# ScalarE copies a chunk's flipped activations before the next chunk's sigmoid, in a decoder layer with 32 experts

## The reference

```python
def clamped_swiglu(gu):
    gate, up = gu[..., :D_FF], gu[..., D_FF:]
    gate = jnp.minimum(gate, SWIGLU_LIMIT)
    up = jnp.clip(up, -SWIGLU_LIMIT, SWIGLU_LIMIT)
    return (up + 1.0) * (gate * jax.nn.sigmoid(gate * SWIGLU_ALPHA))

def expert_block(args):
    xblk, e = args
    act = clamped_swiglu(xblk @ w_gate_up[e] + b_gate_up[e])
    return act @ w_down[e] + b_down[e]
```

## Time and profile before

| what | before |
|---|---|
| median of 3 runs | 1429.55 us (1427.65 to 1431.92) |
| the profiled execution | 1427.33 us, span 1425.6 us |
| TensorE matmul busy | 1286.2 us, 90% of the span |
| VectorE busy | 496.2 us, 35% |
| ScalarE busy | 324.7 us, 23% |
| mean share of granted TensorE clock | 0.958 |
| the main weight queue's packets | 430.86 MB, 74.5% of 16 DMA engines' span |

### The profile page before, as it was taken

The page is one execution under the profiler, slowest core; times in us unless marked ns, Lnnn a source line. Parts: engine busy times, 40 slices in busy tenths (PEclk is TensorE's granted clock), DMA queues, the critical chain, the costliest instruction groups (busy, mean ns, idle before and its releaser), DMA issues.

```text
span 1425.6 us, 33985 instructions
## 1 busy us (share of the span) xinstructions
PE 1286.2 (90%) x12484; PEld 560.1 (39%) x12485; DVE 496.2 (35%) x1476; ACT 324.7 (23%) x649; POOL 299.4 (21%) x348
## 2 busy tenths in 40 slices
PE   6999999959998999999999999888999899988870
PEld 3764544543333434444444333333443333433320
DVE  2002222443334333333333344342334333343337
ACT  2023332221312222222222222221223222222211
POOL 0513332011212212222212112130212212111210
PEclk9999999969999999999999999999999999999995
DMA  9512110224999999999989999998999989999967
GB/s 379 208 59 74 60 74 1 104 83 173 415 386 415 394 413 395 368 365 366 366 366 365 392 418 416 417 416 352 366 367 417 413 362 414 393 417 416 417 248 294
DMA packets 90869, 454.86 MB, mean 319 GB/s; under 512 B 14049, under 2 KB 14489, under 8 KB 55774
## 3 DMA queue, kind: packets, MB, share of 16 engines
q1 hardware_dynamic: 77902, 430.86, 74.5%
q0 software_dynamic: 12512, 22.11, 4.3%
q10 hardware_dynamic: 432, 1.57, 0.3%
HBM read 444.23 MB, written 14.71 MB: 322 GB/s over the span
## 4 chain that ended last, share of the span: by engine, by line
PE 73%; DMA 21%; DVE 3%; issue 1%; ACT 1%; POOL 0%; SPq 0%; DVEq 0%; POOLq 0%
PE bank L661 35%; DMA arena<-in_w_gate_up 20%; PE bank L687 14%; PE bank L421 7%; PE bank L491 4%; PE bank L437 3%; PE bank L648 2%; PE bank L626 2%; PE bank L706 1%; PE bank L450 1%; DVE xs L1284 1%; PE bank L478 1%; PE bank L464 1%; PE bank L707 1%; PE bank L616 1%
## 5 line engine op out<-in xcount | busy, mean ns | idle before, releaser
L661 PE MATMUL bank<-arena,hT 128*32 128x512 f32 x5120 | 583.9, 606 | 30.2 <-DMA arena<-in_w_gate_up 27.9
L687 PE MATMUL bank<-arena,hT 128*32 128x256 f32 x5120 | 308.4, 386 | 33.1 <-ACT hT L859 33.1
L661 PEld LDWEIGHTS bank<-arena,hT 128*32 128x32 f32 x5120 | 157.3, 111 | 393.0 <-issue 341.1
L1241 DVE TENSOR_TENSOR arena<-bank,gain 128x512 f32<-128x512 f32 x128 | 88.4, 691 | 402.0 <-PE bank L661 402.0
L687 PEld LDWEIGHTS bank<-arena,hT 128*32 128x32 f32 x5120 | 159.6, 111 | 161.3 <-issue 77.3
L963 POOL DMA_DIRECT2D ahead<-in_consts x98 | 51.6, 530 | 641.1 <-DVE hT L1260 615.3
L876 ACT ACTIVATE arena<-arena 128x256 f32<-128x256 f32 x128 | 53.3, 417 | 560.1 <-DVE arena L1243 558.7
L1260 DVE TENSOR_TENSOR hT<-bank,gain 128x256 f32<-128x256 f32 x128 | 51.4, 422 | 212.2 <-PE bank L687 206.1
L980 POOL DMA_INDIRECT y_rows<-hT,arena x80 | 82.4, 1029 | 158.3 <-DVE hT L1260 150.7
L421 PE MATMUL bank<-hT,arena 128*128 128x512 f32 x224 | 103.6, 610 | 0.8 <-ACT hT L764 0.8
L966 POOL DMA_INDIRECT hT<-h_rows,arena x82 | 84.8, 1035 | 67.9 <-issue 34.0
(11 more groups left out here) (146 smaller groups left out, 857.9 us busy)
## 6 DMA issues: line engine op xcount, KB each, us to landing
arena<-in_w_gate_up SPq DMA_DIRECT2D x256, 1024.0 KB, 6.6
arena<-in_w_down SPq DMA_DIRECT2D x128, 1024.0 KB, 15.3
arena<-in_w_in SPq DMA_DIRECT2D x10, 1024.0 KB, 18.1
arena<-y_rows SPq DMA_DIRECT2D x8, 1024.0 KB, 12.3
arena<-in_w_out SPq DMA_DIRECT2D x4, 1024.0 KB, 22.0
arena<-bias_by_dist POOLq DMA_DIRECT2D x6, 512.0 KB, 4.0
xs<-in_x SPq DMA_DIRECT2D x4, 512.0 KB, 7.4
h_rows<-arena POOLq DMA_DIRECT2D x4, 512.0 KB, 2.9
```

The source lines that it names most:

```text
L661: mm = pe.matmul(bank[c][j * CH:(j + 1) * CH, :].rearrange("p (g n) -> p g n", g=2), xT[:, c, (k % 2) * P + (k // 2) * CH:(k % 2) * P + (k ...
L687: mm = pe.matmul(bank[c][j * CH:(j + 1) * CH, 0:Q], aT[:, c, (k % 2) * P + (k // 2) * CH:(k % 2) * P + (k // 2 + 1) * CH], w[:, j * Q:(j + ...
L1241: dve.tensor_tensor(gu[:, b, :], bank[c][:, :], bt[:, 0:2 * Q], ALU.add).then_inc(gu_read, 1)
```

## The change

In ScalarE's loop over chunks, the copy of the flipped activations of chunk n - 1 stands ahead of the sigmoid of chunk n, in place of behind it. Nothing else differs; the copy of the last chunk (n = 3) still follows the loop.

```diff
                 for n, c in enumerate(ORDER):
+                    if n >= 1:
+                        copy_act(job, n - 1)
                     act.wait_ge(gate_clamped, job * NCH + (n + 1))
                     act.activation(sg[:, c % 2, :], gu[:, c % 2, 0:Q], ACT.Sigmoid, scale=ALPHA)\
                         .then_inc(sig_done, 1)
-                    if n >= 1:
-                        copy_act(job, n - 1)
                 copy_act(job, NCH - 1)
```

## The result

| | before | after |
|---|---|---|
| median of 11 runs each, taken together | 1427.14 us (1421.17 to 1431.92) | 1433.05 us (1426.63 to 1437.48) |
| ratio | | 1.0046, 95% interval 1.0025 to 1.0067 |
| the profiled execution's span | 1425.6 us | 1428.8 us |

The kernel is 0.46% slower, about 6 us (3.6 to 9.6 us by the interval). The profiled executions are only 3.2 us apart, since the first unit load of the job loop happens to be issued 2.55 us earlier after, behind stages that the change doesn't touch. From there to the end it takes 5.8 us more.

What follows compares the result with a forecast made beforehand. The prediction had TensorE's matmuls and weight transfers bound the loop in turns. It summed 1427.33 - 1.47 (last job) + 1.57 (one clock fall) = 1427.4, plus 2.2 for the runs' median, 1429.6 us; range 1424.0 to 1436.0.

Steps and rivals of the forecast that it cites:

- five places: Ends of full-queue stretches before three-chunk jobs, with no clock fall before; their waits would grow to 2.8 to 3.1 us.
- slower rival: TensorE's clock falls at most of the five places, costing 7.9 to 10.7 less 1.47 us: 1436.0 to 1438.8 us; chance 0.14.
- half-clock stretches behind several of the eight landings: Sign of being wrong: TensorE at 1.2 GHz behind several landings that end full-queue stretches, with a time near 1436.
- (a): ScalarE: three 0.37 us copies move ahead of sigmoids and delay none, with 1.4 us of cover; price nothing.
- (b): TensorE, two-chunk jobs: the 2.05 us copy wait goes, a flip wait of some 0.5 us comes; 1.47 us gained, 16 times.
- (c): Of 16 gains on TensorE, full weight transfers hide 15; only the last job's 1.47 us reaches the end.
- the landing of the eighth gate unit stays where it is: In full-queue stretches this weight landing doesn't move, so TensorE waits there 1.47 us more; gain 0 for 15 jobs.
- (d): Longer TensorE waits for the eighth unit may bring its clock down: 1.25 falls or five, 7.9 to 10.7 us for five.
- one fall at 1.57 us: The clock term taken into the sum, between ends of no fall and five falls.
- The chain's three places: Rival: all three copies on the profile's chain count, 7.7 us faster, 1421.9 us; chance 0.07.
- the full 23.5 us: Rival: all 16 TensorE waits count, needing a queue that TensorE's down pace moves: 1406.1 us; chance 0.03.
- No effect at all: Rival: TensorE's wait comes back in full at the flip, with neither gain nor new falls: 1429.55 us; chance 0.06.

Runs made afterwards that it cites:

- e1_chunk1_alone: Kernel before, with only chunk 1's copy (the third) moved ahead of a sigmoid: 1433.31 us, ratio 1.0044.
- e5: Kernel before, loading only half of each gate-and-up unit from the second job on, so outputs are not the reference's: 1386.29 us.
- e6: Changed kernel, loading only half of each gate-and-up unit from the second job on, so outputs are not the reference's: 1350.86 us.
- e8: Kernel before, with GpSimd's gathers held until VectorE has read the gate of chunk 1: 1426.01 us, ratio 1.0004.
- e12: Changed kernel with 2.8 us of unread matmuls ending two-chunk jobs, as in e7, and gathers held: 1427.09 us, ratio 0.9994.
- e2: Changed kernel, with about 1.5 us of unread matmuls on TensorE where two-chunk jobs had waited for the copy: 1427.62 us, ratio 1.0006.
- e3: Changed kernel, with about 1.5 us of unread matmuls behind down(0), ending two-chunk jobs: 1427.55 us, ratio 1.0008.
- e7: Changed kernel, with about 2.8 us of unread matmuls behind down(0), ending two-chunk jobs: 1425.05 us, ratio 0.9995.
- e9: Changed kernel, first job written out, unread matmuls filling waits for gate units 6 and 7 behind two-chunk jobs: 1443.9 us, ratio 1.0117.
- e10: Control for e9: same added code, but one 16-column matmul in each of the two places: 1441.14 us, ratio 1.0099.
- e4_late_gather: Changed kernel, with GpSimd's gathers held until VectorE has read the gate of chunk 1: 1428.92 us, ratio 1.0016.

## Why the prediction was partly right

**The forecast itself.** It had about no change as the likeliest and the falls of the clock at most of five places as the rival on the slow side. The measured 1433.05 us lies inside the stated bounds of 1424.0 to 1436.0, and that is in part luck: the forecast stood on a median of three runs of the kernel before, 1429.55 us, and eleven gave 1427.14. As a change the forecast was +0.1 us and the slower rival +6.4 to +9.2, and +5.9 was measured. Of its five places three fell, and its own sign of being wrong, half-clock stretches behind several of the eight landings, was seen behind five of seven and in the last job. So the mechanism that it had as a rival is the larger part of what happened.

**(a) ScalarE** was right. No sigmoid is late. The copy that decides is the third; e1_chunk1_alone shows that the others don't count.

**(b) TensorE** had the right mechanism and a gain a little too small. In the last job, after, VectorE's multiply ends and the flip starts 0.06 us later, where I had put 0.24:

```profile
1381.56 0.42 DVE L1249 TENSOR_TENSOR gain<-arena 128x256 f32<-128x256 f32 x1
...
1382.04 0.44 PE L648 MATMUL bank<-cst,gain 128*128 128x128 f32 x2 [0.54 <-DVE gain L1249]
```

The last gate ends at 1379.83 in the chain, so the flip comes 2.21 us behind it. Before it came 1254.46 - 1250.55 = 3.91 us behind it: 1.70 us gained, not 1.47. e5 and e6 bear it out, with 1.65 to 1.75 us in each job where the clock stayed up: 16 x 1.70 = 27.2 us of their 35.4, and the other 8 us are what five falls of the clock cost, where the profiled execution had six.

**(c) What reaches the end** was right in its main claim, that transfers hide 15 of the 16 and that the last one counts. With half the gate loads the gain is 35 us, with whole ones there is none; from the release of the last job's unit 7 to the end it is 60.4 us before and 59.0 after. One step of it failed: "the landing of the eighth gate unit stays where it is". It came 0.4 to 0.6 us later in the stretches with one two-chunk job, 2.2 us in all. It isn't so in the longer stretches 5 and 6. What failed is the premise in (a) that nobody else is queued there: GpSimd's queue keeps its order but not its time. TensorE's earlier arrival lets GpSimd issue the gathers 1.7 us earlier, and about 100 more of their packets come ahead of unit 7 in stretch 2, in a stretch where the DMA engines are full. Over the nine traces of the table above the landing comes later with this count, but for 0.1 to 0.2 us, and where the count is unchanged, in stretches 5 and 6, it stays. Holding the gathers couldn't show it, since that brings others into the stretch.

**(d) The clock** was the right mechanism with the wrong size, and this is the term that the sum fell short by. "I take one fall at 1.57 us" stood for what measured 4.9 us in the profiled execution, three ends more than before and longer stretches at 1.2 GHz in one. I had the new waits as two of 1.2 and 1.6 us; they were 1.1 and 2.4, since the gathers come between units 6 and 7. That the sum of the waits doesn't decide is also shown: in stretch 1 after, three waits of 1.15, 1.70 and 1.62 us had no fall. The same kernel can have more or fewer falls in another execution: over the 11 runs of the changed kernel time and mean granted clock go together, from 1426.63 us at 0.960 to 1437.48 at 0.952. Not all of this spread need be the falls in the loop, since the loop's first unit load was issued anywhere from 334.4 us (e8) to 342.8 us (e12) in the profiled executions, behind stages that are the same in all.

The Trainium skill ("TensorE: Matmul & The Clock Gate", section "HAM oscillation — how this bites in real kernels") describes a kernel whose matmuls for one tile are shorter than the wait for the next operand, and which is throttled again at every tile. The traces agree in kind, with five of seven ends after and all seven in e1_chunk1_alone, but not at each.

**How much is shown.** That ScalarE's new order costs nothing by itself, and that TensorE's earlier arrival makes the loss, is shown by e2, e3 and e7: with the time filled, the ratio goes from 1.0046 to 1.0006, 1.0008 and 0.9995 (the interval of the second just touches that of the changed kernel, the other two don't). That the falls are the larger part of the loss and the later landings the smaller is read from the stretches of one execution each, where a fall makes 9.7 us into 10.2 to 12.5. No run separates the two: the trial that was to show the falls alone, e9 against e10, was spoilt by its own added code and a filler that was too long, and the kernels with held gathers don't take the gathers out of the stretches.

**The rivals.** The chain's three places and the full 23.5 us fell: e5 and e6 show what the second needs. No effect at all fell, as the new wait is 0.54 us and not 2.05. The slower rival came true in its mechanism, with three of its five places and a gain at one that fell before, and the later landings added 2.2 us that it didn't have.

## What to carry to other kernels

A stall on one engine that lies inside a stretch bound by transfers isn't free to remove: the engine only arrives earlier and waits elsewhere. For TensorE, ask where the idle time goes. Moved to just ahead of the landing from which TensorE sets the pace, it can bring the clock down exactly where each matmul counts; left where the transfers have time in hand, the same fall costs nothing. Work put at the end of the short jobs, even useless work, cost nothing that could be told in this kernel, up to 2.8 us a job. Ask as well which small transfers an engine that arrives earlier sets off: in a full queue they come ahead of the weights that everything waits for. And before a run is taken as a test of that, look whether the transfers that it holds back are gone from the stretch, or only others in their place.

## What the runs showed of the hardware

Idle time of 2.0 to 2.5 us in one piece was enough for TensorE to be granted 1.2 GHz behind it, at some places and not at others; the piece of the path behind it grew from 9.71 us to between 10.2 and 12.5 us. Two shorter pieces were enough as well: in e4_late_gather the clock fell behind waits of 1.56 and 1.43 us with 1.06 us of matmuls between them. A fall that nothing hid cost about 1.6 us (e5_before_half_gates). Some 100 to 150 more packets of GpSimd's queue ahead of a 1 MB unit in a full stretch went with a landing 0.4 to 0.6 us later (before and after). Reading one more register per job on TensorE held up the next matmul by 0.7 us (21.4 us over 31 jobs), and the first pass through code written out a second time held TensorE up by 5.21 and 4.45 us, once. VectorE hands over to TensorE in 0.06 us, ScalarE in 0.24 to 0.28.
